# High and low weight halves interleaved word by word for TensorE's weight loads

## What is computed

```
h = rmsnorm(x, norm_mix_pre[l])
proj = h @ w_in[l]
...                                   # mixers; y @ w_ret_out, w_sc_out, w_cf_out
x = x + rmsnorm(merged @ w_o[l], norm_mix_post[l])
h = rmsnorm(x, norm_ffn_pre[l])
up = causal_dwconv(h @ w_up[l], ffn_conv_w[l])
gate, val = jnp.split(up, 2, axis=-1)
x = x + rmsnorm((silu(gate) * val) @ w_down[l], norm_ffn_post[l])
```

## Time and profile before

| | |
|---|---|
| median of 3 runs | 3190.43 us (3190.35 to 3190.72) |
| profiled execution, its own time | 3190.44 us |
| its span | 3189.1 us |
| matmuls in the profile | 14964 |
| granted clock of TensorE, mean | 0.999 |

### The profile page before, as it was taken

One profiled execution on the slowest core, in us unless ns is written; L12 is line 12 of the kernel. 1 busy time (PEld: TensorE's weight loads), 2 busy tenths in 40 slices (PEclk: granted clock), 3 DMA queues, 4 the chain that ended last, 5 costly groups with the idle time before them and its releaser, 6 DMA issues.

```text
span 3189.1 us, 37007 instructions
## 1 busy us (share of the span) xinstructions
PE 3169.5 (99%) x14964; PEld 2654.6 (83%) x14964; DVE 1835.7 (58%) x2469; ACT 1243.9 (39%) x1866; POOL 396.0 (12%) x293
## 2 busy tenths in 40 slices
PE   8999999999999999999999999999999999999999
PEld 7888888888888888888888888888888888888887
DVE  6875456665687545656557543447545754345744
ACT  3332334344333233434445422236534442224642
POOL 0201212210020121211011000110012000011001
PEclk9999999999999999999999999999999999999999
DMA  4322223235442222323532222222232132222222
GB/s 167 116 99 93 99 93 112 94 132 188 139 125 93 99 93 100 106 97 119 194 125 78 97 99 87 97 86 98 97 122 87 67 104 94 86 99 95 92 94 101
DMA packets 100232, 339.71 MB, mean 107 GB/s; under 512 B 12288, under 2 KB 12544, under 8 KB 99296
## 3 DMA queue, kind: packets, MB, share of 16 engines
q1 hardware_dynamic: 96736, 322.76, 29.8%
q0 software_dynamic: 3184, 14.06, 1.3%
q10 hardware_dynamic: 144, 0.52, 0.1%
HBM read 326.29 MB, written 2.10 MB: 103 GB/s over the span
## 4 chain that ended last, share of the span: by engine, by line
PE 97%; DVE 1%; issue 1%; ACT 0%; DMA 0%; POOL 0%; POOLq 0%
PE ps L500 96%; PE ps L605 1%; PE ps L844 0%; DVE r L1427 0%; DVE wl L1417 0%; DMA X<-x_in 0%; POOL sm L2020 0%; ACT f L1265 0%; DVE h L1560 0%; DVE sm L1853 0%; PE ps L555 0%; DVE f L1553 0%; DVE f L1803 0%; DVE f L1863 0%; DVE r L1835 0%
## 5 line engine op out<-in xcount | busy, mean ns | idle before, releaser
L500 PE MATMUL ps<-h,wh 128*128 128x512 f32 (+1 forms) x5824 | 1702.5, 376 | 2.2 <-DVE h L1560 1.8
L500 PEld LDWEIGHTS ps<-h,wh 128*128 128x128 f32 x5824 | 1066.8, 189 | 199.3 <-issue 4.6
L500 PE MATMUL ps<-h,wl 128*128 128x512 f32 (+1 forms) x2912 | 1093.2, 375 | 0.0
L1417 DVE TENSOR_TENSOR wl<-raw,wh 128x1024 fp32r<-128x1024 f32 (+3 forms) x596 | 751.8, 1272 | 319.6 <-ACT wh L957 318.7
L957 ACT CAST wh<-raw 128x1024 fp32r<-128x1024 f32 (+3 forms) x596 | 595.9, 1008 | 720.1 <-PE ps L500 718.3
L500 PEld LDWEIGHTS ps<-h,wl 128*128 128x128 f32 x2912 | 548.7, 188 | 98.8
L500 PE MATMUL ps<-r,wh 128*128 128x512 f32 x1632 | 503.8, 390 | 0.0
L500 PEld LDWEIGHTS ps<-r,wh 128*128 128x128 f32 x1632 | 305.2, 188 | 62.7
L500 PE MATMUL ps<-r,wl 128*128 128x512 f32 x816 | 317.5, 389 | 0.0
L1032 ACT CAST r<-f 128x512 fp32r<-128x512 f32 x186 | 114.6, 620 | 511.9 <-DVE f L1756 148.5
L500 PE MATMUL ps<-wh,r 128*128 128x512 f32 x960 | 302.6, 390 | 0.3
(11 more groups left out here) (152 smaller groups left out, 2085.9 us busy)
## 6 DMA issues: line engine op xcount, KB each, us to landing
raw<-wst SPq DMA_DIRECT2D x544, 512.0 KB, 3.3
raw<-wst SPq DMA_DIRECT2D x48, 320.0 KB, 2.8
f<-gains POOLq DMA_DIRECT2D x6, 1024.0 KB, 5.2
raw<-wst SPq DMA_DIRECT2D x16, 384.0 KB, 3.0
f<-f SPq DMA_DIRECT2D x72, 64.0 KB, 2.0
f<-tab POOLq DMA_DIRECT2D x16, 256.0 KB, 5.0
r<-r SPq DMA_DIRECT2D x32, 128.0 KB, 2.3
X<-x_in SPq DMA_DIRECT2D x4, 512.0 KB, 8.4
```

What stands on the lines that cost most here:

```text
L500: return e.matmul(o, a, b, start=start, stop=stop, skip_group_check=True)
L1417: e.tensor_tensor(l[:, 0:WIDTH[c]], raw[:, c % NRAW, 0:WIDTH[c]], h[:, 0:WIDTH[c]].bitcast(F32), ALU.subtract).then_inc(*lo_cut.up(("lo", c)))
```

## The change

One ring `ws` takes the place of `wh` and `wl`. A slot (`SLOT`) is 2 x 1024 + 64 words, 8448 bytes = 33 x 256. `WAY` is 16 words, so a slot starts 174208 = 680.5 x 256 bytes from `base`.

- Chunks that are loaded: word 2n of the slot is high part n, word 2n + 1 is low part n. Each part is read and written with a step of two words, and starts 128 bytes (the low part 132) from the activations modulo 256.
- Chunks that are streamed: they start 32 words (128 bytes) into the slot, high part and then low part, contiguous. They lie at the same place modulo 256 as the activations, as before.
- The 20 kept chunks stay in the arena.

```diff
-WAY = 48
+
+WAY, SLOT = 16, 2 * CH + 64
+STREAMED = ("wo", "dn", "vb", "va", "v")
+
+
+def streamed(c):
+    return CHUNKS[c][0].split("/")[1].rstrip("0123456789_") in STREAMED
...
-        wh = sb("wh", [P, WAY + NSP * CH], F32R)
-        wl = sb("wl", [P, NSP * CH], F32R)
+        ws = sb("ws", [P, WAY + NSP * SLOT], F32R)
...
-            n = RING[c] % NSP * CH
-            return wh[:, WAY + n:WAY + n + CH], wl[:, n:n + CH]
+            n = WAY + RING[c] % NSP * SLOT
+            if streamed(c):
+                return ws[:, n + 32:n + 32 + CH], ws[:, n + 32 + CH:n + 32 + 2 * CH]
+            turns = ws[:, n:n + 2 * CH].rearrange("p (n two) -> p n two", two=2)
+            return turns[:, :, 0], turns[:, :, 1]
```

## The result

The changed kernel takes 3237.38 us (3237.34 to 3238.09) against 3190.39 us for the kernel before: ratio 1.0148, 95% interval 1.013 to 1.0165, so 47 us slower. The forecast was 3068 us.

A forecast was written before the change was run, and what follows sets the result against it. TensorE's pace through its matmuls was taken as the bound. From 3190.4 us, 120 (512-column) and 10 (256-column matmuls with loaded weights) came off and 8 was given back: 3068 us, range 3047 to 3200.

The forecast's parts named there:

- The bound: Whole kernel: time can only be won in TensorE's pace through 14964 matmuls; it is busy 3169.5 of 3189.1 us.
- What the 13.3 ns are: Each float32r matmul: 13.3 ns over its columns, 6%, come from load and stream reads getting in each other's way.
- term 1: Matmuls with loaded weights: a two-word step gives load and stream one pace; -120 us at 512 columns, -10 at 256.
- The float32 row: Plain float32 matmuls: load and stream go at one pace and pay 1.3 ns, taken as the price after the change.
- It meets the load in every position wherever it starts: Float32r matmuls before the change: the stream, twice as fast, slides past the load through every position modulo 256.
- Terms 2 and 3: Streamed weights and kept chunks stay at 226.7 ns; `ct` in the transposes moves to 64 bytes above the activations: nothing.
- Term 4: Cuts on ScalarE and VectorE write, and VectorE also reads, with a step of two words: no change taken.
- Term 5: Faster TensorE runs into VectorE, transfers and chains at layer boundaries: 8 us given back, including settling after interruptions.
- Nothing happens: Rival, chance 0.10: the 13.3 ns of float32r matmuls are a switching cost; time stays 3190 us.
- Half a cure: Rival, chance 0.15: only half the price of loaded-weight matmuls goes, 67 us and up to 10; 3115 to 3125 us.
- A load with a step runs at half pace: Rival, chance 0.10: loads take 218 ns, so 256-column matmuls go from 120 to 218: 3303, or 3190 to 3200 us.
- The step costs more than the meeting did: Rival, chance 0.15: each 16 bytes a load touches takes a stream cycle; 240 ns a matmul, +149 us, 3339 us.

The follow-up runs named there:

- one_word_128: Changed kernel with the parts of loaded chunks contiguous again, still 128 bytes from the activations modulo 256: 3245.20 us, ratio 1.0172.
- one_word_0: Changed kernel, still with one ring, but loaded chunks contiguous and at distance 0 like the streamed ones: 3190.99 us, ratio 1.0002.
- parked stream: Kernel of matmuls alone, without the computation, whose moving operand reads one word over and over: 215.8 ns a matmul against 226.7 for 512 words.
- maps of distances: Kernels of matmuls alone, without the computation, with loads at many steps and distances modulo 256: two-word steps take 230.0 to 233.4 ns.

## Why the prediction was wrong

- **The bound** was right: TensorE's pace per matmul decides, and nothing else moved. The loss is the change of pace times the number of matmuls, 45 + 2 us, against 47 measured.
- **"What the 13.3 ns are" is the step that failed**, in its conclusion "two reads that get in each other's way would", and with it term 1 of the sum (-120 and -10 us; measured +45 and +2). The observation under it was good: the price comes and goes with the offset in time. But I read a price that depends on timing as a price that load and stream owe to their meeting. A load that stands still, or is a quarter as long, leaves 231 to 232 ns; a stream that stands still leaves 215.8. The price needs the stream's movement over 64 bytes or more and does not need the load's; the load's place and step decide what is paid on top: 226.7 ns at best, elsewhere between 228 and 240. So load and stream do act on each other, but moving them apart was no cure. Whether a moving stream would pay with no load at all, no run shows.
- **The float32 row** The earlier trace rows was the wrong neighbour. I took its 1.3 ns as the fruit of equal pace. With float32 the load's step and place change nothing at all (429.2 ns in four forms), so the row said nothing about equal pace. What I read as two matmuls are the two records of one, and the 1.3 ns came from a duration rounded to 10 ns: measured over 190 spacings it is 2.5.
- **"It meets the load in every position wherever it starts"** is contradicted by one_word_128: the place alone is worth 55 us, with every step left at one word.
- **Terms 2 and 3** (streamed weights, `ct`) were right: 227.4 to 227.5 ns, and one_word_0 equals the kernel before. **Term 4** was right for VectorE (1307 ns both times) and wrong for ScalarE (+6%), whose slack hides it. **Term 5** had no occasion.
- **The rivals.** "Nothing happens" missed the time by 47 us, and its switching cost of 13.3 ns is 2.5 ns by the parked stream. "Half a cure" did not come: with a step of two no place of the maps of distances is below 230.0 ns. "A load with a step runs at half pace" did not come either: the 256-column matmuls still start 120 ns apart, not 218. "The step costs more than the meeting did" came out on the right side with the wrong mechanism: 240 ns was asked for at every distance, measured were 230.0 to 233.4 on the map and 231.5 in the kernel, and two words cost nothing beside a parked stream. A loss by leaving a good place was not among my rivals, though the profile held a hint: spacings all at 226 or 227 ns, between values of 224 to 236 after each interruption, are a rhythm that something could break.
- **The Trainium skill.** "TensorE: Matmul & The Clock Gate", Part 2, step 1, gives the load a read port of its own that takes nothing from the running matmul. Beside a parked stream the rows agree: loads of step 1 and 2 are free. Beside a moving stream they do not: the load's place alone moves the pace from 226.7 to 232.5 ns, and the time that I had derived from the rule, 3190 us, was missed by 47. The measurement decides. The same page of the Trainium skill, Part 1, "Wait — 56ns, not 53.3ns?", has a warm spacing of 215.7 ns for 512 columns. It is met by the parked stream (215.8) and by no moving float32r stream here (226.7 or more). The Trainium skill's page "SBUF — State Buffer", section "Door 1: The DMA port swizzle", wants two accesses to each 16-byte line. The loads beside a parked stream agree: two words per line are free, one word per line costs 17.5 ns. The stream with a step of two also makes two accesses per line and does not agree: it takes twice as long.

Open: why a stream pays once it covers 64 bytes, why the best rhythm is 32 cycles above the columns, and why 0 and 120 bytes find it, 112 and 128 don't, and 16 does only at times. No run looks inside a matmul. What is shown is that the place and the step of the loaded operand, relative to the moving one, make the loss; how they do it is not shown.

## What to carry to other kernels

When a matmul costs a few per cent more than its columns, look at the single spacings before explaining the mean: a constant one can be a settled rhythm between load and stream, which a change of address may break. The place modulo 256 bytes was worth 1.7% here with contiguous weights, and place and step together up to 2.2%, with the same order of instructions. So a re-layout of weights should keep the distance and the step that it had, or be tried at several distances, and it should leave the streamed operand contiguous. And a neighbour in the trace only prices a mechanism if the mechanism acts in it: here float32 did not care about its loads at all.

## What the hardware showed that I had not expected

- With the same 14964 matmuls, the addresses alone (place and step of the weights) moved the kernel between 3189.88 and 3261.70 us.
- Both operands moved together by 32, 64 or 128 bytes keep 226.7 ns, so the place that counts is a relative one; 8 bytes of it can be worth 6 ns (120 against 128 bytes).
- A float32r stream confined to 32 bytes runs at 215.8 ns, in a window of 64 bytes at 241.8, slower than over the whole tile (226.7).
- A float32r stream with a step of two words takes 451 to 453 ns for 512 columns, twice the contiguous one.
- At a distance of 16 bytes one kernel holds 226.7 ns for hundreds of matmuls in some stretches and 233.3 in others.
- ScalarE writes float32r with a step of two words 6% slower (1111 against 1046 ns for 1024 words); VectorE shows no difference at 1307.
